# Where the prompt's compressed attention, the gates, the trailing means and the samples' selection are computed in a one-core decoder layer

## The reference, cut to what matters

```
h = rmsnorm(x) * (1 + scale1(c)) + shift1(c)
nq, nkv, ng, mlstm columns, pool columns = split_cols(h @ w_in)
# NSA: three branches, mixed by gates g = sigmoid(ng)
kc, vc = compress(rows)           # 32 rows weighted by wpos, then @ cmp_w + cmp_b, stride 16
s_c = q . kc * scale;  p_c = masked_softmax(s_c, cmp_end <= qpos);  o_c = p_c @ vc
imp = p_c summed over a group's heads and over the 4 (+1) blocks of a 64-row block
top, idx = top_k(where(forced, 1e6, imp), 16);  o_s = masked_softmax(q . ks[idx]) @ vs[idx]
o_w = masked_softmax(q . kw) @ vw                      # the last 512 rows
o   = g0 * o_c + g1 * o_s + g2 * o_w
# mLSTM: 4 heads with matrix memory C, chunks of 64;  pool: means over 2/4/8/16 rows, then a linear map
x = x + gate1(c) * (concat(nsa, mlstm, pool) @ w_out)
x = x + gate2(c) * ((silu(a) * b) @ w_down),  [a, b] = conv3(rmsnorm2(x) @ w_up)
```

## Time and profile of the kernel before

| what | value |
|---|---|
| three runs | 878.70, 880.62 and 887.47 us, median 880.62 |
| profiled execution | 877.8 us, its span 876.0 us |
| mean granted TensorE clock in it | 0.945 of full speed |
| busy in the span | PE 796.2 us (91%), DVE 496.5, ACT 329.0, POOL 299.3 |

### The profile page before, as it was taken

How to read it: one execution, slowest core, us unless ns; L and a number is a source line. 1 busy time by engine, 2 the same in 40 slices (tenths; PEclk the granted TensorE clock), 3 DMA queues, 4 the chain that set the end, 5 groups by cost and what they waited for, 6 DMA issues and landing times.

```text
span 876.0 us, 18827 instructions
## 1 busy us (share of the span) xinstructions
PE 796.2 (91%) x7553; PEld 727.5 (83%) x7553; DVE 496.5 (57%) x987; ACT 329.0 (38%) x601; POOL 299.3 (34%) x147
## 2 busy tenths in 40 slices
PE   2899999989986588998997999999999999999994
PEld 2798889977865455666996999999999999999993
DVE  3725677661267978875377466666211666666224
ACT  4432232323130255664234544554112444554221
POOL 0044546540000033444341334443444334443440
PEclk9999999998586689998999999999999999999997
DMA  9956788766269444403361233333223333222212
GB/s 352 324 199 191 244 271 270 241 203 184 74 216 346 118 115 119 125 14 140 131 229 49 85 122 109 111 119 101 89 88 109 112 118 104 90 97 91 82 64 98
DMA packets 72549, 130.19 MB, mean 149 GB/s; under 512 B 12612, under 2 KB 47308, under 8 KB 72208
## 3 DMA queue, kind: packets, MB, share of 16 engines
q1 hardware_dynamic: 66336, 113.27, 40.1%
q10 hardware_dynamic: 6096, 15.73, 5.4%
q0 software_dynamic: 32, 0.00, 0.0%
HBM read 123.52 MB, written 9.11 MB: 151 GB/s over the span
## 4 chain that ended last, share of the span: by engine, by line
PE 66%; DVE 14%; DMA 6%; SPq 6%; issue 4%; POOL 2%; ACT 2%; DVEq 0%; ACTq 0%; POOLq 0%
PE ps L654 49%; SPq L471 4%; DMA arena<-cache_keys 4%; PE ps L980 2%; PE ps L995 2%; PE ps L1016 2%; POOL arena L600 2%; PE ps L1030 2%; DVE arena L1478 1%; DMA arena<-weights 1%; PE ps L874 1%; DVE arena L1479 1%; DMA raw<-weights 1%; DVE arena L1475 1%; DVE arena L2038 1%
## 5 line engine op out<-in xcount | busy, mean ns | idle before, releaser
L654 PE MATMUL ps<-hR,wR 128*128 128x260 f32 x3456 | 426.6, 285 | 12.0 <-POOL wR L620 5.0
L654 PEld LDWEIGHTS ps<-hR,wR 128*128 128x128 f32 x3456 | 420.2, 190 | 17.2 <-issue 8.6
L620 POOL TENSOR_TENSOR wR<-raw,wR 128x1024 fp32r<-128x1024 f32 x92 | 222.4, 2418 | 291.6 <-ACT wR L1112 291.6
L1112 ACT ACTIVATE wR<-raw 128x1024 fp32r<-128x1024 f32 x94 | 99.4, 1058 | 214.9 <-PE ps L654 207.1
L654 PE MATMUL ps<-fR,wR 128*128 128x260 f32 x1056 | 128.1, 283 | 2.2 <-DVE fR L2009 2.0
L654 PEld LDWEIGHTS ps<-fR,wR 128*128 128x128 f32 x1056 | 127.0, 188 | 3.1 <-DVE fR L2009 2.4
L2033 DVE COPY arena<-arena 128x2 f32<-128x2 f32 x44 | 47.7, 1083 | 93.6 <-ACT arena L1404 93.6
L612 POOL TENSOR_SCALAR arena<-arena,fac 128x128 f32<-128x128 f32 (+3 forms) x32 | 42.8, 1339 | 165.7 <-DVE fac L1932 165.6
L600 POOL TENSOR_TENSOR arena<-arena,par 128x1024 f32<-128x1024 f32 x16 | 33.6, 2098 | 96.1 <-DMA arena<-cache_keys 96.1
L1994 DVE TENSOR_TENSOR t<-ps,mod 128x8 f32<-128x8 f32 x24 | 4.0, 167 | 108.0 <-PE ps L654 108.0
L1475 DVE TENSOR_REDUCE arena<-arena 128x64 f32<-128x1024 f32 x16 | 19.5, 1218 | 43.7 <-POOL arena L600 43.7
(11 more groups left out here) (369 smaller groups left out, 863.8 us busy)
## 6 DMA issues: line engine op xcount, KB each, us to landing
raw<-weights SPq DMA_DIRECT2D x95, 512.0 KB, 3.7
arena<-cache_keys SPq DMA_DIRECT2D x128, 192.0 KB, 3.4
arena<-weights SPq DMA_DIRECT2D x27, 512.0 KB, 9.6
arena<-cache_values SPq DMA_DIRECT2D x128, 64.0 KB, 1.9
raw<-weights ACTq DMA_DIRECT2D x12, 512.0 KB, 6.5
arena<-weights ACTq DMA_DIRECT2D x9, 512.0 KB, 7.3
x<-xT SPq DMA_DIRECT2D x16, 260.0 KB, 4.2
out_y<-x SPq DMA_DIRECT2D x8, 260.0 KB, 2.2
```

The lines of the kernel that those rows point to most:

```text
L620: nc.gpsimd.tensor_tensor(w_slot(i)[:, 1, :, :], raw[:, g % RAW, :, :], w_slot(i)[:, 0, :, :].bitcast(F32), ALU.subtract).then_inc(lo_read ...
L654: last = mm(ps[:, a + half, 0:TH], w_slot(i)[:, wp, k, :], src[:, hp, j, half * TH:(half + 1) * TH], start=(j == 0 and q == 0), stop=(j == ...
L1112: A(w_slot(i)[:, 0, :, :], raw[:, g % RAW, :, :], ACT.Identity).then_inc(hi_ready, 1)
```

## The change

It moves four groups of work out of the matrix-memory stage, and rewrites that stage's order on PE, ACT and DVE.

1. **Into the input projection, on PE**: the transposes of the prompt's gates (p = 6), the product for the prompt's compressed keys (p = 11) and the compressed scores of query group r (p = 12 to 15). They use free columns of PSUM bank 5, the bank of `blocks`, so they and `blocks` wait for each other's evacuations.
2. **Into the projection, on DVE**: both `trailing_sums`, the second of the prompt's sums earlier, four `prompt_cmp_scores`, the softmax's maximum, the gates and the softmax's weights. ACT gets the gates' exponential, the keys' evacuation and the softmax's exponential (p = 17). The multiplication with `cmul` (0 where a block isn't visible) is gone: the maximum is instead kept from falling under NEG/10.
3. **The samples' selection** comes in front of `exponents(1)` and `states(0)`. The maximum over 64-row blocks of the unmasked scores (`bmax`) is taken beforehand, so that after the selection a maximum over 40 columns replaces the one over 2056.
4. **In the flips**: the softmax's factors are no longer multiplied into `sall`, `swin` and `scm`, but into three diagonal matrices (`flat`) of 64 x 64, and the 23 transposes become 23 matmuls with these.

The core of the diff (L-numbers of the rows after the change are those of the changed file):

```diff
@@ events
+        if p == 6:
+            out.append(("gates",))
+        if p == 17:
+            out.append(("pexp",))
...
+            if p == 11:
+                out.append(("keys",))
+            if 12 <= p < 12 + G:
+                out.append(("csc", p - 12))
@@ PE, blocks
                     if b:
                         pe.wait_ge(blocks_evac, b)
+                    if b == 0:
+                        pe.wait_ge(side_evac, 1)
+                    elif 3 <= b < 6:
+                        pe.wait_ge(csc_moved, (1, 3, 4)[b - 3])
@@ PE, new steps
+                elif ev[0] == "keys":
+                    pe.wait_ge(psum_ready, 1)
+                    pe.wait_ge(blocks_evac, 3)
+                    mm(ps[:, 5, 384:384 + NCP], par_("cw", 0, P), psum4[:, 0, 0, 0:NCP], start=True, stop=True).then_inc(side_done, 1)
+                elif ev[0] == "csc":
+                    r = ev[1]
+                    pe.wait_ge(side_evac, 2)
+                    pe.wait_ge(blocks_evac, (3, 4, 4, 5)[r])
+                    if r:
+                        pe.wait_ge(csc_moved, r)
+                    for i in range(ST):
+                        at = P + i * 2 * NCP
+                        last = mm(ps[:, 5, at:at + 2 * NCP], pT[:, r, i * P:(i + 1) * P], kct[:, 64:64 + 2 * NCP], start=True, stop=True)
+                    last.then_inc(csc_done, 1)
@@ PE, flips
                 for c in range(NPG):
-                    nc.tensor.transpose(ps[:, 4 + c // 8, (c % 8) * 64:(c % 8 + 1) * 64], sall[:, c * P:(c + 1) * P],
-                                        ident[0:64, 0:64])
+                    mm(ps[:, 4 + c // 8, (c % 8) * 64:(c % 8 + 1) * 64], sall[:, c * P:(c + 1) * P], flat[:, 64:128], start=True, stop=True)
@@ DVE, loop over the cached pages
                     half_sums(h)
+                    if b in (4, 5):
+                        prompt_cmp_scores(h - 8)
...
-                if b == 1:
+                if b == 0:
+                    trailing_sums(0)
+                elif b == 1:
                     gate_rows()
+                elif b == 2:
+                    prompt_sums(0)
+                    prompt_sums(1)
                 elif b == 3:
-                    prompt_sums(0)
+                    trailing_sums(1)
                 elif b == 4:
                     gate_sums()
                 elif b == 5:
-                    prompt_sums(1)
+                    prompt_cmp_max()
                 elif b == 6:
                     gate_maxima()
...
+                    prompt_gates()
+                elif b == 7:
+                    prompt_cmp_weights()
@@ DVE, samples
-            for r, (n, buf) in enumerate(((8, sall[:, :]), (5, swin[0:64, 0:T]))):
...
-                last = V.tensor_scalar(buf, buf, ssx[:, 12 + r:13 + r], None, ALU.mult)
...
+            V.tensor_scalar(flat[:, 64:128], ident[0:64, 0:64], ssx[:, 10:11], None, ALU.mult)
```

More of the change, by code:

```diff
@@ L780, in _ @@
             last.then_inc(kn_T, 1)
+            pe.wait_ge(rows_ready, 1)
+            for i in range(ST):
+                last = nc.tensor.transpose(ps[:, 1, P + i * 96:P + (i + 1) * 96], grow[0:96, i * P:(i + 1) * P], ident[0:96, 0:96])
+            last.then_inc(r_T, 1)
             for c, t in enumerate([T_MQ, T_MQ + 1, T_MK, T_MK + 1, T_G]):
@@ L791, in _ @@
-            pe.wait_ge(rows_ready, 1)
-            pe.wait_ge(sn_evac, 1)
-            pe.wait_ge(pooled_ready, NB + 2)
-            for h in range(NH):
-                mm(ps[0:64, 2, 400:403], pick[:, 7 - h:71 - h], sn[0:NB, 6 * P + 64 + 3 * h:6 * P + 67 + 3 * h], start=(h == 0), stop=(h == NH - 1))
-            for i in range(ST):
-                last = nc.tensor.transpose(ps[:, 2, i * 96:(i + 1) * 96], grow[0:96, i * P:(i + 1) * P], ident[0:96, 0:96])
-            last.then_inc(r_T, 1)
+            pe.wait_ge(psum_ready, 2)
@@ L887, in _ @@
             row_broadcast(0)
+            triple(0)
             chunk_scores(0)
[L889 to L895 removed]
@@ L904, in _ @@
-            chunk_scores(1)
-            pe.wait_ge(sn_evac, 1)
-            for c in range(4 * ST):
-                r, i = c // ST, c % ST
-                at = (c % 8) * 2 * NCP
-                last = mm(ps[:, r // 2, at:at + 2 * NCP], pT[:, r, i * P:(i + 1) * P], kct[:, 64:64 + 2 * NCP],
-                          start=True, stop=True)
-            last.then_inc(csc_done, 1)
+            gate_columns()
+            sample_rows()
+            block_sums()
+            row_broadcast(1)
+            window_scores(0)
@@ L937, in _ @@
+            across(3)
             triple_turn(4)
             triple(5)
-            across(2)
-            across(3)
+            pe.wait_ge(pool_ready, 1)
+            pe.wait_ge(num_evac, 4)
+            for t in range(2):
+                mm(ps[:, t, :], par_("pw", t * P, (t + 1) * P), md[:, t, :], start=True, stop=True)
+                last = mm(ps[:, 6, t * NB:(t + 1) * NB], par_("pw", t * P, (t + 1) * P), mds[:, t, :], start=True, stop=True)
+            last.then_inc(pool_mm, 1)
             triple_turn(5)
@@ L947, in _ @@
             last.then_inc(hT_done, 1)
-            pe.wait_ge(pool_ready, 1)
-            for t in range(2):
-                mm(ps[:, t, :], par_("pw", t * P, (t + 1) * P), md[:, t, :], start=True, stop=True)
-                last = mm(ps[:, 6, t * NB:(t + 1) * NB], par_("pw", t * P, (t + 1) * P), mds[:, t, :], start=True, stop=True)
-            last.then_inc(pool_mm, 1)
             triple_turn(6)
@@ L1234, in step @@
                     A(lfo[0:4, :], lfo[0:4, :], ACT.Ln, bias=1.0).then_inc(ln_ready, 1)
+                elif ev == ("gates",):
+                    act.wait_ge(side_done, 1)
+                    A(gN[:, :, :], ps[:, 5, P:P + 96].rearrange("p (i n) -> p i n", i=ST), ACT.Exp, scale=-1.0).then_inc(side_evac, 1)
+                elif ev == ("keys",):
+                    act.wait_ge(side_done, 2)
+                    for g in range(2):
+                        last = A(kct[hr[g], 64 + g * NCP:64 + (g + 1) * NCP], ps[hr[g], 5, 384:384 + NCP], ACT.Identity,
+                                 bias=par_("bk", lo=hr[g].start, hi=hr[g].stop))
+                    last.then_inc(side_evac, 1)
+                elif ev == ("pexp",):
+                    act.wait_ge(pcx_ready, 1)
+                    A(pc[:, :, 0:NCP], pc[:, :, 0:NCP], ACT.Exp).then_inc(pcx_exp, 1)
             for ev in [("lin", 16), ("lin", 17)] + EVENTS:
@@ L1819, in _ @@
[L1819 to L1824 removed]
+            samples_output_gates()
```

308 lines of the change are left out of this document (157 added, 151 removed).

## The result

The changed kernel takes 892.68 us (median of 4 runs, 891.33 to 896.43) against 879.66 us before (873.25 to 887.47); the ratio is 1.0167, with a 95% interval of 1.0129 to 1.0204. It is slower, by 13 us or 1.7%. Its profiled execution took 891.3 us, with a span of 889.5 us, 13.5 us more than the span of 876.0 us before.

The account below looks back on a forecast made before the run. PE was taken to bound the projection, and PE at 1.2 GHz, then DVE, the matrix-memory stage. 10.9 + 2.9 - 13.7 + 6.8 = +6.9 on 877.8 gave 884.7, or 887.5 on the median's scale; range 870 to 899.

Parts of the forecast that it names:

- A: Input projection: grows by 10.9 us, from 4.2 of moved PE work plus three stops totalling 9.0, less one old stop of 2.3.
- B: Input projection: the clock falls behind two of the three new stops, 1.4 us each, costing 2.9 us.
- C: Matrix-memory stage: shrinks by 13.7 us, with units starting at 288.0 instead of 301.7.
- D: Flips: 23 matmuls in place of transposes cost 6.8 us more, mostly reckoned at the lower clock level.
- the walk: Matrix-memory stage: C's five-step passage through the new order, from the last broadcast to the units' start at 288.0.
- step 1: Start of C's walk: PE's last broadcast moves from 249.5 to 244, with about 2.5 us of waits for the window's rows.
- The rival in which the stops don't show: Projection: no new stops, A only 1.9 and B nothing; -5.0 us, 872.8 or 875.6; chance 15%.
- the one at the upper level: Matrix-memory stage comes up to the upper clock level: C 27.7, D 2.3, sum -11.6, 866.2 or 869.0; chance 17%.
- the one at the lower level throughout: Matrix-memory stage stays at the lower clock: C only 2.7, sum +19.8, 897.6 or 900.4; chance 18%.

Follow-up runs that it names:

- x2: Changed kernel with ACT evacuating the blocks ahead of its four DMA issues at an odd item instead of behind them; 881.8 us, ratio 1.0014.
- x1: Changed kernel with the keys' product at p = 10 and compressed scores at p = 12, 14, 16, 18, one item behind a blocks step; 879.42 us, ratio 0.9992.
- y4: Kernel before, with the five early output DMAs issued only after the last triple; 887.48 us, ratio 1.0079.
- x3: Changed kernel with three of ACT's four DMA issues ahead of the blocks' evacuation and one behind it; 886.32 us, ratio 1.0069.
- y3: Changed kernel with the samples' selection and its exponential back behind states 1, the small maximum kept; 901.7 us, ratio 1.0226.
- x7: x1 with the five early output DMAs issued only when all eight triples are evacuated; 868.36 us, ratio 0.9861.
- y1: x7 with transposes in the flips and the five outputs issued behind the first two loads of window values; 871.62 us, ratio 0.9899.
- x4: Changed kernel with part four undone: transposes in the flips, factors multiplied into the samples' weights by DVE; 886.12 us, ratio 1.0061.
- x5: Kernel before with part four alone: factors in diagonal matrices, 23 matmuls in place of 23 transposes; 887.76 us, ratio 1.0082.

## Why the prediction was right, and where its terms were off

The forecast was 887.5 us in a range of 870 to 899, with slower by over 1% at 0.38 and within 1% at 0.48; measured was 892.7 us, inside the range, and slower by 1.7%. The class it held likeliest, within 1%, did not come. On the traces' scale the sum said +6.9 and the spans say +13.5, twice that: of the 6.6 us between them 4.9 are A and B together, 3.2 the first stage, and C, D and the rest take 1.5 back. The causes were mostly right and one size was not. By its steps:

- **A, +10.9.** The stops were foreseen at 3 x 3.0 and measured at 9.2, at the three foreseen places, with ACT's issues as cause (x2). The work at the upper level was foreseen at 4.2; x1 shows 3.8 net. The stop at 189.68 is gone as foreseen, and the reason given, the lead from the stops, fits: in x2, without the long stops, PE waits 2.85 us at the same item. Missed: POOL's weights are late by 0.95 and 0.47 us at 108 and 125 us; I had priced such effects at nothing. Before had one such stop of 0.85 us, so 0.6 net. POOL had been waiting for a load of cached keys (6.90 us at 103.86); whether DVE's new work made it late is not shown, since y4, with before's order on DVE, has stops of 1.64 and 1.42 us of this kind.
- **B, +2.9, the step that failed.** It took two falls of three and 1.4 us each. The level was down behind all three; the three items behind them took 5.3 us more (7.52, 7.98 and 7.83 against 6.02), and the two score groups 0.8 us each more, which the step had left out: 6.9. The argument from a stop of 2.34 us that left the clock alone fell with x3, x2 and y4. A and B together are 18.7 in the traces, not 13.8.
- **C, -13.7.** Measured -12.8, or -14.3 from the same point as in the walk (the mods' wait, 301.76 before and about 309.4 after). Seen from the stage's first turn (208.1 in the walk's time), the walk's marks and the trace's are: last broadcast 35.9 and 32.5 us, selection's end 46.4 and 42.4, first head result 53.2 and 52.4, last head result 67.3 and 69.5, first unit 79.9 and 79.4. The order of causes was right (y3), and of the two new waits of 2.6 us step 1 had one, the window's rows; the other, ahead of triple 1, stood only in a rival. The agreement of the sum owes something to chance: x7 and y1 show that the same order of the stage takes 67 to 79 us as the clock falls out.
- **D, +6.8.** The flips grew by 6.95 us, and the path from the mods' wait to the step behind the flips by 6.6 (7.54 and 14.2 us); undone they give 6.6 (x4), done alone they cost 7.6 (x5). The factor of 3.6 from the rows was a little low: sixteen transposes alike took 1.70 us from start to start (304.42 to 306.12) and sixteen matmuls 6.73 (311.88 to 318.61), 4.0 times, the flips in all 3.7 times. The matmuls did not raise the clock: it is 0.50 over their 9.5 us. The Trainium skill (Perfetto Trace Analysis, section Transposes) asks for a transpose instead of a standard matmul wherever one is meant; the 9.5 us against 2.6 agree.
- **Not in the sum.** The first stage was 3.2 us longer in this trace. x5 and y4, which run before's code there, also start later than before's profile (73.29 and 72.17 against 71.96), so that part of the 3.2 is an execution's own. The eleven traces with the changed code have 73.94 in the middle, against 72.17 in the three of before; with one trace of each version, whether the changed kernel is later on average stays open.

The rival in which the stops don't show is refuted; the one at the upper level came true only in mended versions (x7, whose stage is 24.6 us shorter than before's, and by its times half of y1's executions); the one at the lower level throughout describes two thirds of the stage, for which the walk had already allowed.

## What to carry to other kernels

Where a row shows an engine busy all through a stretch, ask of each instruction added there not its length but what it waits for, and what stands on the releasing engine ahead of the release: here 4 us of matmuls cost 19 because they stood right behind a result whose evacuation lay behind four DMA issues, and one item later they cost 4. A stop of PE in dense work is to be priced above its length: here stops of 9.2 us brought 6.9 us of lower clock with them. And when a mended version is earlier, look for the transfers that were just in time before.

## What the runs showed of the hardware that I had not expected

- Stops in the otherwise dense projection of 1.65 (y1), 1.98, 2.05, 2.23, 2.28, 2.35 and about 3.0 us were followed by 1.2 GHz for most of an item (7.3 to 8.0 us instead of 6.0); stops of 0.5, 1.64 (y4), 1.70 (y1) and 2.34 us (before) were not. At the same item of the same code 2.34 us left the level up (before) and 2.05 brought it down (y4), so in this range the length alone does not tell; what else decides was not tried.
- The granted clock stayed at 0.50 for 51 us with PE busy for 46 of them, and the same instructions came back to 1.00 at 257 us in one kernel and after 277 in another, for 11.8 us of time. What in this stretch keeps the level down was not tried.
- Five output DMAs and `out_spool`, issued from 258 to 262 us, held up a 512 KB load of another queue to 15.8 us from issue to landing, against 6.6 at most without them (x1 and x7). From 255 to 285 us of x1 2651 of 5488 packets are under 512 B, which fits small packets as the cause; the size itself was not varied.
